# Moving GpSimd's four full-row operations from the second to the fifth pair of experts

## The reference, cut to what matters

```python
for layer in range(DEPTH_2):
    ...                                   # mixer: dilated, then stick-breaking attention
    x = layer_norm(DEEPNORM_ALPHA * x + mixed, ln1_g[layer], ln1_b[layer])
    ffn = moe_ffn(x, router_w, router_b, exp_w_gate[layer], exp_w_up[layer], exp_w_down[layer])
    x = layer_norm(DEEPNORM_ALPHA * x + ffn, ln2_g[layer], ln2_b[layer])

def layer_norm(x, g, b):
    xf = x.astype(jnp.float32)
    mu = xf.mean(-1, keepdims=True)
    var = jnp.square(xf - mu).mean(-1, keepdims=True)
    return ((xf - mu) * lax.rsqrt(var + LN_EPS) * g + b).astype(x.dtype)

def expert_block(args):                   # in moe_ffn: 16 experts in 4 groups, two chosen for a token
    xi, e = args
    return (jax.nn.silu(xi @ w_gate[e]) * (xi @ w_up[e])) @ w_down[e]
```

## Time and profile before

| | us |
|---|---|
| median of three timed executions | 1367.08 |
| lowest and highest of them | 1366.31, 1368.42 |
| the profiled execution | 1365.09 |
| its span, first to last instruction | 1363.3 |
| TensorE busy | 1300.8 (95%) |
| VectorE busy | 938.8 (69%) |
| ScalarE busy | 712.5 (52%) |
| GpSimd busy | 95.0 (7%) |

### The profile page before, as it was taken

One profiled execution on the slowest core, in us unless ns is written; L12 is line 12 of the kernel. 1 busy time (PEld: TensorE's weight loads), 2 busy tenths in 40 slices (PEclk: granted clock), 3 DMA queues, 4 the chain that ended last, 5 costly groups with the idle time before them and its releaser, 6 DMA issues.

```text
span 1363.3 us, 18226 instructions
## 1 busy us (share of the span) xinstructions
PE 1300.8 (95%) x7375; PEld 723.7 (53%) x7384; DVE 938.8 (69%) x1132; ACT 712.5 (52%) x760; POOL 95.0 (7%) x56
## 2 busy tenths in 40 slices
PE   6999999989999989999999999999989989999996
PEld 4686555446654445555557556444445555644443
DVE  5686776877764586464658576766867666678586
ACT  5466565345543364353456446555635673756462
POOL 0000000000000012000024002000004000300000
PEclk9999999999999999999999999999999999999999
DMA  9474434645655655564720235787936403569692
GB/s 319 136 248 157 152 124 155 224 170 186 211 206 189 240 189 198 172 236 159 249 96 1 74 135 166 260 286 254 365 128 231 171 1 124 186 197 328 215 342 91
DMA packets 152652, 258.09 MB, mean 189 GB/s; under 512 B 8881, under 2 KB 81532, under 8 KB 152572
## 3 DMA queue, kind: packets, MB, share of 16 engines
q1 hardware_dynamic: 152572, 256.97, 56.1%
HBM read 255.88 MB, written 1.07 MB: 188 GB/s over the span
## 4 chain that ended last, share of the span: by engine, by line
PE 81%; DVE 8%; DMA 4%; ACT 3%; issue 2%; DVEq 1%; POOL 1%; SPq 0%; ACTq 0%; POOLq 0%
PE ps L1215 13%; PE ps L1031 12%; PE ps L749 11%; PE ps L730 8%; PE ps L1033 6%; PE ps L1054 6%; PE ps L1294 6%; DVE w_ring L1923 4%; PE ps L767 3%; PE ps L991 2%; DMA w_ring<-in_exp_w_up 2%; PE ps L1271 1%; ACT w_hi L1489 1%; PE ps L694 1%; PE ps L1151 1%
## 5 line engine op out<-in xcount | busy, mean ns | idle before, releaser
L1923 DVE SCALAR_TENSOR_TENSOR w_ring<-w_ring,w_hi 128x2048 f16<-128x2048 f32 (+2 forms) x206 | 464.6, 2267 | 158.0 <-ACT w_hi L1489 156.8
L1489 ACT ACTIVATE w_hi<-w_ring 128x2048 f16<-128x2048 f32 (+2 forms) x206 | 381.6, 1864 | 225.1 <-PE ps L1054 50.9
L1031 PE MATMUL ps<-actT,w_hi 128*128 128x512 f16 x640 | 209.0, 380 | 0.7 <-issue 0.7
L1033 PE MATMUL ps<-actT,w_ring 128*128 128x256 f16 x640 | 174.8, 273 | 0.0
L749 PE MATMUL ps<-w_hi,actT 128*128 128x512 f16 x448 | 135.9, 379 | 2.9 <-DVE w_ring L1923 2.9
L1489 ACT ACTIVATE arena<-ps 128x256 f16<-128x256 f32 (+7 forms) x85 | 59.4, 709 | 143.9 <-PE ps L1033 77.1
L1215 PE MATMUL ps<-w_hi,arena 128*128 128x512 f16 x432 | 134.3, 379 | 0.0
L1215 PE MATMUL ps<-w_ring,arena 128*128 128x512 f16 x352 | 133.4, 379 | 0.0
L730 PE MATMUL ps<-w_hi,actT 128*128 128x512 f16 (+2 forms) x384 | 112.9, 371 | 2.8 <-DVE actT L1928 2.8
L1031 PEld LDWEIGHTS ps<-actT,w_hi 128*128 128x128 f16 x640 | 62.8, 98 | 77.4 <-issue 2.4
L1215 PE MATMUL ps<-arena 128*128 128x512 f16 x272 | 84.5, 379 | 3.8 <-DVE arena L2708 3.8
(11 more groups left out here) (430 smaller groups left out, 1934.2 us busy)
## 6 DMA issues: line engine op xcount, KB each, us to landing
w_ring<-in_dil_w_in SPq DMA_DIRECT2D x36, 1024.0 KB, 5.2
w_ring<-in_w_ff SPq DMA_DIRECT2D x32, 1024.0 KB, 5.1
w_ring<-in_exp_w_gate SPq DMA_DIRECT2D x64, 512.0 KB, 4.4
w_ring<-in_exp_w_up SPq DMA_DIRECT2D x64, 512.0 KB, 5.5
w_ring<-in_exp_w_down SPq DMA_DIRECT2D x32, 1024.0 KB, 5.7
w_ring<-in_w_in SPq DMA_DIRECT2D x24, 1024.0 KB, 5.1
w_ring<-in_sb_w_in SPq DMA_DIRECT2D x12, 1024.0 KB, 5.9
w_ring<-in_w_branch SPq DMA_DIRECT2D x8, 1024.0 KB, 5.0
```

What stands on the lines that cost most here:

```text
L1031: pe.matmul(ps[:, bank + c, :], w_h[:, k, cols], aT[:, kk, :], start=(kk == 0), stop=False, skip_group_check=True)
L1033: ins = pe.matmul(ps[:, bank + c, 0:S], w_l[:, k, cols], aT[:, kk, 0:S], start=False, stop=(kk == KD - 1), skip_group_check=True)
L1489: return act.activation(dst, src, ACT.Copy, scale=scale)
L1923: dve.scalar_tensor_tensor(out=lo16(h)[:, 0:kn * c], in0=w_ring[:, h % RING, 0:kn * c], scalar=W_POW, in1=hi16(h)[:, 0:kn * c], op0=ALU.mu ...
```

## The change

GpSimd's wait for `w_lo` ahead of `full` becomes a wait for 24 halves of the expert layer instead of 8, in both expert layers (m = 0 and m = 2). The call for m = 1 keeps its wait. No operation is added or removed, and the order of each queue stays.

```diff
                 if m < 3:
                     pool.wait_ge(sig("ld_gb"), 16 + 32 * (m + 1))
-                    pool.wait_ge(sig(("w_lo", "qkv_out", "w_lo")[m]), (2 * MOE0 + 8, 22, 2 * MOE1 + 8)[m])
+                    pool.wait_ge(sig(("w_lo", "qkv_out", "w_lo")[m]), (2 * MOE0 + 24, 22, 2 * MOE1 + 24)[m])
                     full((6, 7, 8)[m], True)
```

## The result

The changed kernel takes 1368.80 us in the median of 22 executions (1366.50 to 1373.33), the kernel before 1366.99 in as many (1365.22 to 1369.53). The ratio is 1.0018, with a 95% interval of 1.0011 to 1.0025: slower by 0.18%, or 2.5 us (1.5 to 3.4). The medians lie only 1.8 us apart; the means of the 22 lie 2.5 us apart, as the ratio has it. The change goes the way of the forecast, and the median is 1.8 us under its 1370.6.

What follows compares the result with a forecast made beforehand. The prediction took TensorE to bound the kernel (81% of the chain that ended last), GpSimd counting only where TensorE waits. Its terms, -4.1 + 5.3 + 2.3 = +3.5 us on the median 1367.08, gave 1370.6 us, range 1367.4 to 1373.8.

Steps and rivals of the forecast that it cites:

- The mechanism: GpSimd beside VectorE operations with two SBUF inputs: whole instructions exclude each other, first come first, then alternating; turns 2.16 and 2.20 us.
- What the change removes: TensorE's waits for L2708 at the old place go in both expert layers: 1.97 + 2.17, so 4.1 us gained.
- The bound of 0: Old place: the other end of the gain term, 0 if a second release stood right behind.
- What it adds, first layer: New place, first expert layer: GpSimd goes first, held splits delay weigh and h_low, down products come 5.3 us late.
- Second layer: New place, second expert layer: the split goes first, down products come 2.3 us late; 4.4 if GpSimd first.
- Who goes first: New threshold: GpSimd wins in the first layer by 0.13 us and loses in the second by 0.23.
- rivals 1 and 2: Both expert layers: 1, GpSimd first in both, +5.6 us, chance 0.27; 2, the split first in both, +1.4, chance 0.12.
- Rival 5: Same expert layers: later waits for late weights shrink by what is added, +0 to +1 us, about 1367.5; chance 0.10.
- The sum: Whole execution: -4.1 + 5.3 + 2.3 = +3.5 us, on the median 1370.6 us.

Runs made afterwards that it cites:

- without the rows: Against the kernel before: GpSimd's two multiplies and two additions replaced by a one-element multiply at the old threshold, in both expert layers; ratio 0.9960, -5.5 us.
- third trace: The changed kernel run once more with nothing else changed, a third look at who goes first; single time 1368.82 us.
- the first layer alone: Against the kernel before: the new threshold (24 halves) in the first expert layer only, the old one in the second; ratio 1.0025, +3.4 us.
- two places: Against the kernel before: GpSimd's multiplies wait for the 14th half and its additions for the 32nd, both expert layers; ratio 0.9951, again 0.9943.
- at 32: Against the kernel before: the threshold for all four GpSimd operations at 32 halves in both expert layers; ratio 0.9956, -6.0 us.
- the split first: Against the changed kernel: GpSimd waits for the h_low between the two splits, so the split behind it has begun; ratio 0.9996 to the kernel before.
- the second layer alone: Against the kernel before: the new threshold (24 halves) in the second expert layer only; ratio 0.9999.

## Why the prediction was right, and where it was off

- **The mechanism** (whole turns, first come first served, only for two SBUF inputs) held in every row: splits at 4.04 to 4.43, PSUM operations unchanged. The 2.22 us for an unhindered GpSimd turn, for which the prediction gave no row, came back: GpSimd at 902.03 and the held split's end at 906.53, less its own 2.28, leave 2.22.
- **What the change removes**, 4.1 us: -2.1 and -1.9 without the rows, 4.0. The bound of 0 did not come up.
- **What it adds, first layer**, +5.3 with GpSimd first: net +3.3 expected, +3.2, +3.1 and +3.2 in the stretch. The path inside was a little different: in the first two traces the wait for the split is missing and that for h_low is 1.35, not about 2, and in both TensorE ran part of these products at the lower clock (granted clock 0.89 from 903 to 918; 1.00 in the third trace, with waits of 0.94 and 1.92). The stretch was the same in all three, so inside a wait the lower clock cost nothing.
- **Second layer**, +2.3 with the split first: net +0.2 expected, +0.2, +0.2 and -0.0 measured. The wait for a split was to be about 1 and is 0.32 at most; it drops out of the sum, since h_low's wait of 1.93, forecast as about 2, ends last.
- **Who goes first**: GpSimd in the first layer, the split in the second, as forecast from GpSimd's own starts. The 0.48 us of the second layer came back as 0.47 (1251.43 + 4.50 = 1255.93, then 1256.40) and was no accident: every trace but one in which the end of a split or of an h_low lets these multiplies of the second layer go has 0.47 or 0.48 (ten after a split, one after an h_low). The one exception has 0.14, and it is the kernel without the rows, whose instruction there is another. Why it is more than in the first layer (0.13 to 0.14) no run shows. The recorded start is what counted: at 902.03 GpSimd held back the split recorded at 902.15. The step was right, and rivals 1 and 2, whose orders the experiments did produce (+4.7 and +1.1 in the stretches), did not occur.
- **Rival 5**, part given back later, is out: the down products of the fourth pair were 5.29 late, 3.3 net of the old wait, and the stretch that ends in the seventh pair still has +3.2; the kernel with the first layer alone has +3.1 there.
- **The sum** was +3.5; the stretches give +3.2 to +3.4, the times +2.5 (1.5 to 3.4) and +2.9 (1.5 to 4.2), so the shortfall is hardly more than the intervals allow. What the sum had no term for is the rest of the execution, with its steps of 1.7 us whose number differs between executions. That they made the shortfall is not shown: the mean clock of the changed kernel is, if anything, lower than that of the kernel before, which alone would make it slower, not faster. I gave 0.65 to slower by over 0.2% and 0.26 to within; the ratio of 0.18% falls just within. The weak point was to treat +3.5 as if only the three runs' scatter stood between it and the median.
- **What stays open**: why the kernels with less delay in the first layer gained 1.5 to 3.9 us more than their stretches show (no rows 5.5 against 4.0, two places 6.7 against 4.2 and 7.8 against 3.9, at 32 6.0 against 2.7, and the split first 0.5 gained against 1.1 lost). Their traces lack a slow piece near 1015 us, and their mean clock is higher, but no run here changes the clock alone; that the placement of TensorE's waits decides it is a guess, and the trace with the second layer alone, which lacks the piece too, speaks against it as the whole cause.

## What to carry to other kernels

GpSimd's work on large SBUF tiles is not free beside VectorE: each instruction can hold back a VectorE operation with two SBUF inputs, and all that is queued behind it. So choose its place by VectorE's queue: find a stretch where VectorE is idle or has only operations with a PSUM input, and where the next two-input operation has a late user; here that turned a cost of 4 us into none that could be measured, while a move by sixteen halves to a place that looked no busier cost 3 us more. And work out a change of a few us in stretches between two fixed operations, since the rest of the execution moves by more than that.

## What the runs showed of the hardware that was not expected

- GpSimd's start after the end of the split that releases it was 0.13 to 0.14 us in the first expert layer and 0.47 to 0.48 in the second, for the same line, in both the kernel before and the changed one. With a competing start 0.26 us away in the first layer and 0.25 in the second, this decided who went first, and the order is worth about 2 us (+2.9 against +1.1 in the first layer's stretch, +1.8 against -0.0 in the second's).
- A lead of 0.12 us in the recorded start was enough to go first, three times out of three. Where the order changed between two traces of one kernel (8.64 against 6.70 us for the same two multiplies), VectorE had come 0.22 us ahead in the one and 0.35 behind in the other.
- TensorE's granted clock has short pieces at 1.2 GHz, at places that differ between executions of one kernel, most worth 1.7 us where TensorE is busy throughout, 0.8 near 303 us where it partly waits, and nothing in the fourth pair of the first layer, inside a longer wait.
